# A two-layer diffusion backbone on one core: half-width sweeps ahead of the wide norms

## The reference

```python
def rms_norm(x, g):
    y = xf * lax.rsqrt(jnp.mean(xf * xf, axis=-1, keepdims=True) + EPS)
    return (y * g.astype(jnp.float32)).astype(x.dtype)
def swiglu(h, wg, wu, wd):
    return (jax.nn.silu(h @ wg) * (h @ wu)) @ wd
# layer
ada = lambda t, g, shift, scale: rms_norm(t, g) * (1 + scale) + shift
x = x + 0.5 * m(2) * ffn(ada(x, lp['norm_ffn1'], m(0), m(1)), 'ffn1')     # and xc, the context
y, yc = token_mix(ada(x, lp['norm_mix'], m(3), m(4)), ada(xc, ...), ...)  # w_in, four mixers, merge, w_out
x = x + m(5) * y
x = x + 0.5 * m(8) * ffn(ada(x, lp['norm_ffn2'], m(6), m(7)), 'ffn2')
```

## Time and profile before

| | |
|---|---|
| median of 3 runs | 2421.13 us (2415.59 to 2423.13) |
| profiled execution | 2425.87 us, span 2423.8 us |
| PE busy | 2273.6 us, 94% of the span |
| DVE busy | 1144.6 us, 47% |
| ACT busy | 863.2 us, 36% |
| POOL busy | 165.7 us, 7% |
| HBM | 322.86 MB moved by DMA, mean 133 GB/s |

### The profile page before, as it was taken

How to read it: one execution, slowest core, us unless ns; L and a number is a source line. 1 busy time by engine, 2 the same in 40 slices (tenths; PEclk the granted TensorE clock), 3 DMA queues, 4 the chain that set the end, 5 groups by cost and what they waited for, 6 DMA issues and landing times. The chain is left out here.

```text
span 2423.8 us, 33976 instructions
## 1 busy us (share of the span) xinstructions
PE 2273.6 (94%) x13093; PEld 1806.2 (75%) x13093; DVE 1144.6 (47%) x1847; ACT 863.2 (36%) x1350; POOL 165.7 (7%) x279
## 2 busy tenths in 40 slices
PE   4999998889999989899999989999998999988998
PEld 3777776768766767667777767788776877788997
DVE  1433332376377546543323244333336738775555
ACT  2322222243455442332222233223223446634443
POOL 2000000310000001000000000000013001110000
PEclk8999999989999999999999999999998999988999
DMA  9554636623333335255463635533363435564663
GB/s 270 154 159 113 171 108 184 183 70 90 87 97 100 95 100 164 71 140 166 115 173 110 170 107 140 157 96 96 105 168 80 114 97 147 145 177 140 179 181 110
DMA packets 584420, 322.86 MB, mean 133 GB/s; under 512 B 14666, under 2 KB 576310, under 8 KB 584150
## 3 DMA queue, kind: packets, MB, share of 16 engines
q1 hardware_dynamic: 570368, 288.40, 42.7%
q0 software_dynamic: 12464, 28.32, 4.3%
q10 hardware_dynamic: 1446, 4.18, 0.5%
HBM read 309.72 MB, written 12.94 MB: 133 GB/s over the span
## 5 line engine op out<-in xcount | busy, mean ns | idle before, releaser
L614 DVE TENSOR_TENSOR w_lo<-raw,w_hi 128x1024 fp32r<-128x1024 f32 (+1 forms) x412 | 497.8, 1209 | 1042.0 <-ACT w_hi L604 554.1
L604 ACT ACTIVATE w_hi<-raw 128x1024 fp32r<-128x1024 f32 (+1 forms) x412 | 428.5, 1040 | 966.4 <-PE bank L664 384.1
L663 PE MATMUL bank<-h_hi,w_hi 128*128 128x512 f32 (+1 forms) x1792 | 655.7, 376 | 13.2 <-DVE h_lo L1461 10.5
L664 PE MATMUL bank<-h_lo,w_hi 128*128 128x512 f32 (+1 forms) x1792 | 638.4, 366 | 0.0
L663 PEld LDWEIGHTS bank<-h_hi,w_hi 128*128 128x128 f32 x1792 | 343.1, 191 | 90.6 <-issue 35.2
L669 PE MATMUL bank<-h_hi,w_lo 128*128 128x512 f32 (+1 forms) x1792 | 393.1, 362 | 0.7 <-DVE w_lo L614 0.7
L664 PEld LDWEIGHTS bank<-h_lo,w_hi 128*128 128x128 f32 x1792 | 343.6, 192 | 52.0 <-issue 1.0
L669 PEld LDWEIGHTS bank<-h_hi,w_lo 128*128 128x128 f32 x1792 | 309.8, 190 | 52.2 <-DVE w_lo L614 1.1
L663 PE MATMUL bank<-inner_hi,w_hi 128*128 128x512 f32 (+1 forms) x704 | 254.0, 370 | 8.8 <-DVE inner_lo L1526 5.7
L664 PE MATMUL bank<-inner_lo,w_hi 128*128 128x512 f32 (+1 forms) x704 | 252.1, 368 | 0.0
L678 PE MATMUL bank<-h_hi,w_hi 128*128 128x512 f32 (+1 forms) x512 | 170.3, 351 | 13.2 <-ACT wa L1320 7.7
(11 more groups left out here) (226 smaller groups left out, 2258.7 us busy)
## 6 DMA issues: line engine op xcount, KB each, us to landing
raw<-in_w_mod_dram SPq DMA_DIRECT2D x144, 512.0 KB, 3.9
raw<-in_w_in_dram SPq DMA_DIRECT2D x108, 512.0 KB, 3.8
raw<-in_ffn_w_gate_dram SPq DMA_DIRECT2D x88, 512.0 KB, 4.9
raw<-in_ffn_w_up_dram SPq DMA_DIRECT2D x88, 512.0 KB, 5.0
raw<-in_ffn_w_down_dram SPq DMA_DIRECT2D x64, 512.0 KB, 4.0
raw<-in_ffn_w_down_dram SPq DMA_DIRECT2D x32, 384.0 KB, 3.7
raw<-in_w_branch_dram SPq DMA_DIRECT2D x16, 512.0 KB, 5.4
raw<-in_w_out_dram SPq DMA_DIRECT2D x16, 512.0 KB, 4.4
```

What stands on the lines that cost most here:

```text
L604: act.activation(w_hi[n % 2][:, 0:unit.rows, :], raw[unit.slot][:, 0:unit.rows, :], ACT.Copy).then_inc(hi_made, 1)
L614: dve.tensor_tensor(w_lo[n % 2][:, 0:unit.rows, :], raw[unit.slot][:, 0:unit.rows, :], w_hi[n % 2][:, 0:unit.rows, :].bitcast(F32), ALU.su ...
L663: pe.matmul(psum, w_hi[s][:, row0 + k, :], hi, start=(k == 0), stop=False)
L664: mm = pe.matmul(psum, w_hi[s][:, row0 + k, :], lo, start=False, stop=False)
```

## The change

Four of the six sweeps that a norm follows are done twice over, once for each token half: layer 0's last down sweep of the first block, its output projection, its last down sweep of the second block, and layer 1's last down sweep of the first block. Such a sweep has sixteen steps of 256 columns; the weights are loaded and split again for the second eight. During the second eight the norm of the first token half is worked: its sum after the ninth product, then root and reciprocal, then one chunk in each step. The first two products behind the norm run for the first token half and then for the second, and the sum of the second half stands inside them, after four steps. The adds of squares go to GpSimd, for every norm but the first. The first norm of the kernel is worked in two halves, one after the other. The parts are 8, 6 and 8 chunks, and the modulation units move accordingly. The vectors of the next modulation are made at step 6 of the sweep instead of 5.

```diff
-PARTS = [(0, 8), (8, 8), (16, 6)]
+PARTS = [(0, 8), (8, 6), (14, 8)]
-MOD_AT = {(0, 1, 0): (0, 16, 1), (0, 1, 1): (0, 32, 1), (0, 1, 2): (0, 48, 2),
+MOD_AT = {(0, 1, 0): (0, 16, 1), (0, 1, 1): (0, 32, 2), (0, 1, 2): (0, 56, 1),
...
+HALVED = [(0, (1, 2)), (0, "out"), (0, (2, 2)), (1, (1, 2))]
+def sweep_halves(l, name):
+    return 2 if (l, name) in HALVED else 1
+def sweep_steps(l, name):
+    return DC * sweep_halves(l, name)
...
-        TURN_AT = 5
+        TURN_AT = 6
...
+                        for again in range(sweep_halves(l, (ffn, part))):
+                            stage(first["down", l, ffn, part] + again * DC, DC, lambda j: [((0, n), columns(wd, l, j * P, n, c0))])
...
# TensorE, first_pair
+                for st in streams(n):
+                    cols = stream_cols(st)
+                    last = st == streams(n)[-1]
+                    for step in range(DC + 2):
+                        if (st, step) == (0, 4) and key != (0, 1) and n > LAT:
+                            sum_squares(key, 1)
...
+                            if which == 0:
+                                h_made.wait(pe, (*key, k, st))
+            def sum_squares(key, st):
+                cols = stream_cols(st)
+                (summed if key == (0, 1) else pooled).wait(pe, (key, DC - 2, st))
+                pe.matmul(sum_bank(key, st)[:, cols], const("ones"), wb[:, 1, cols], start=True, stop=False)
+                squares.wait(pe, (key, DC - 1, st))
...
# TensorE, between (after product d of a sweep)
+                if key and (l, name) in HALVED and d == DC:
+                    sum_squares(key, 0)
+                if key and (l, name) not in HALVED and d == DC - 1:
+                    sum_squares(key, 0)
...
# ScalarE, block_splits
+                for d in range(sweep_steps(l, name)):
...
                         act.wait_ge(added, add_first[l, name] + d + 1)
-                        square(key, n, d)
+                        square(key, d % DC, d // DC)
+                        if halved and d == DC:
+                            norm_root(key, 0)
+                        if halved and d >= DC:
+                            norm_hi(key, d - DC, 0)
...
-                norm_block(l, "mix", TOK, 1)
+                norm_block((l, "mix"), range(1, 2))
...
# VectorE, add_block
+                for d in range(sweep_steps(l, name)):
                     split_lo(dve, units[u0 + d].product + 2)
-                    if norm_key and d > 0:
-                        add_square(norm_key, norm_n, d - 1)
...
+                    for st in [d // DC] if halved else streams(n):
...
                     ins.then_inc(added, 1)
+                    if halved and d == DC:
+                        norm_invert(key, 0)
+                    if halved and d >= DC:
+                        norm_scale(key, d - DC, 0)
+                        if d > DC:
+                            norm_lo(key, d - DC - 1, 0)
+                if halved:
+                    norm_lo(key, DC - 1, 0)
...
# GpSimd
+            def add_squares(l, name):
+                key, n = next_norm(l, name)
+                for st in streams(n):
+                    squares.wait(pool, (key, 0, st))
+                    for k in range(1, DC - 1):
+                        squares.wait(pool, (key, k, st))
+                        if k > 1:
+                            pooled.wait(pool, (key, k - 1, st))
+                        before = wa[:, 0, stream_cols(st)] if k == 1 else wb[:, 1, stream_cols(st)]
+                        pooled.done(pool.tensor_tensor(wb[:, 1, stream_cols(st)], before, wa[:, k % 2, stream_cols(st)], ALU.add), (key, k, st))
...
                     load_modulation(0, "rest")
+                    add_squares(0, (1, 2))
                     neighbourhood_bias(0)
                     mixer_transfers(0)
+                    add_squares(0, "out")
```

More of the change, by code:

```diff
@@ L564, in _ @@
                                  ((0, DC), w_branch[l].rearrange("k (c p) n -> p (k c) n", p=P)[:, :, d * P:(d + 1) * P]))
-                        stage(first["out", l], DC, lambda j: [((0, DC), columns(w_out, l, j * P))])
+                        for again in range(sweep_halves(l, "out")):
+                            stage(first["out", l] + again * DC, DC, lambda j: [((0, DC), columns(w_out, l, j * P))])
                     for part, (c0, n) in enumerate(PARTS):
@@ L945, in _ @@
                             pe_start.done(mm, ("x", k))
-                    sum_squares((0, 1), TOK)
+                    for st in range(2):
+                        sum_squares((0, 1), st)
                     turn_modulation(0, "in")
@@ L1083, in _ @@
                 u0, a0 = first["out", l], add_first[l, "out"]
-                for d in range(DC):
+                for d in range(sweep_steps(l, "out")):
                     pe.wait_ge(added, a0 + d - 1)
+                    cols = stream_cols(d // DC) if (l, "out") in HALVED else slice(0, n)
                     if d == 0:
                         merged.wait(pe, (l, 6))
-                    product(u0 + d, 0, (0, 0), (bank[4 + d % 2][:, 0:n], 0, DC, h_rhs(n),
+                    product(u0 + d, 0, (0, 0), (bank[4 + d % 2][:, cols], 0, DC, lambda k: (h_hi[:, k, cols], h_lo[:, k, cols]),
                                                 (lambda k: h_made.wait(pe, (l, "merged", k))) if d == 0 else None))
@@ L1121, in root, with norm_root, norm_hi, norm_block @@
                 roots.done(act.activation(dst, psum, ACT.Sqrt, bias=eps_col[0:psum.shape[0], 0:1], scale=scale), key)
-            def norm_block(l, which, n, mod_i):
-                root((l, which), sums, (l, which), bank[6][:, 0:n], rstd[:, 0:n], 1.0 / D)
-                vectors.wait(act, (l, "in" if mod_i == 0 else "rest"))
-                for k in range(DC):
-                    normed.wait(act, (l, which, k))
-                    for st in streams(n):
-                        cols = slice(st * LAT, (st + 1) * LAT)
-                        ins = act.activation(h_hi[:, k, cols], wa[:, k % 2, cols], ACT.Identity,
-                                             bias=mod[:, 3 * mod_i * DC + k, st:st + 1])
-                    h_hi_made.done(ins, (l, which, k))
+            def norm_root(key, st):
+                root((key, st), sums, (key, st), sum_bank(key, st)[:, stream_cols(st)], rstd[:, stream_cols(st)], 1.0 / D)
+                if key[0] != "final":
+                    vectors.wait(act, (key[0], "in" if key[1] == 1 else "rest"))
+            def norm_hi(key, k, st):
+                normed.wait(act, (*key, k, st))
+                h_hi_made.done(act.activation(h_hi[:, k, stream_cols(st)], wa[:, k % 2, stream_cols(st)], ACT.Identity,
+                                              bias=mod[:, 3 * norm_vectors(key) * DC + k, st:st + 1]), (*key, k, st))
+            def norm_block(key, halves):
+                for st in halves:
+                    norm_root(key, st)
+                    for k in range(DC):
+                        norm_hi(key, k, st)
             def up(l, ffn, part, n):
@@ L1173, in block_splits @@
                 key, n = next_norm(l, name)
-                for d in range(DC):
+                halved = (l, name) in HALVED
+                for d in range(sweep_steps(l, name)):
                     if key and d == 0:
@@ new lines, in add_square_start, with norm_invert, norm_scale @@
+                    summed.wait(dve, ((0, 1), k - 1, 1))
+                    summed.done(dve.tensor_tensor(wb[:, 1, :], wb[:, 1, :], wa[:, k % 2, :], ALU.add), ((0, 1), k, 0))
+                summed.mark(((0, 1), k, 1))
+            def norm_invert(key, st):
+                roots.wait(dve, (key, st))
+                link(dve.reciprocal(rstd[:, stream_cols(st)], rstd[:, stream_cols(st)]))
+            def norm_scale(key, k, st):
+                if k >= 2:
+                    h_hi_made.wait(dve, (*key, k - 2, st))
+                    h_made.wait(dve, (*key, k - 2, st))
+                normed.done(dve.scalar_tensor_tensor(out=wa[:, k % 2, stream_cols(st)], in0=X[:, k, stream_cols(st)], scalar=gain[:, norm_vectors(key), k, st:st + 1],
+                                                     in1=rstd[:, stream_cols(st)], op0=ALU.mult, op1=ALU.mult), (*key, k, st))
@@ new lines, in norm_lo @@
+            def norm_lo(key, k, st):
+                normed.wait(dve, (*key, k, st))
+                h_hi_made.wait(dve, (*key, k, st))
+                h_made.done(dve.scalar_tensor_tensor(out=h_lo[:, k, stream_cols(st)], in0=wa[:, k % 2, stream_cols(st)],
+                                                     scalar=mod[:, 3 * norm_vectors(key) * DC + k, st:st + 1],
+                                                     in1=h_hi[:, k, stream_cols(st)].bitcast(F32), op0=ALU.add, op1=ALU.subtract), (*key, k, st))
@@ L1503, in up, with norm_block @@
+            def norm_block(key, halves):
+                for st in halves:
+                    norm_invert(key, st)
+                    for k in range(DC + 1):
```

(4 more changed lines are left out.)

147 lines of the change are left out of this document (61 added, 86 removed).

## The result

| | before | after |
|---|---|---|
| median (runs) | 2422.07 us (4) | 2438.64 us (4; 2437.79 to 2440.91) |
| profiled execution | 2425.87 us, span 2423.8 | 2439.42 us, span 2437.8 |
| TensorE busy | 2273.6 us | 2285.4 us |
| VectorE, ScalarE, GpSimd busy | 1144.6, 863.2, 165.7 us | 1172.0, 901.8, 210.7 us |
| moved by DMA | 322.86 MB | 339.78 MB |

The ratio is 1.0077, 95% interval 1.0060 to 1.0095. The forecast was +11.6 us; the profiled executions differ by 13.6 and the medians by 16.6. The median forecast was 2433 in a range of 2427 to 2440; 2438.64 lies near its upper end.

A forecast was written before the change was run, and what follows sets the result against it. TensorE was taken as the bound nearly everywhere, except 33.0 us of waits for norms' first chunks. Four halved sweeps with norms +11.3, start norm +3.8, layer 1's last block -3.5: +11.6 us, median 2433, range 2427 to 2440.

The forecast's parts named there:

- The ring of the halved sweeps: VectorE-ScalarE hand-overs pace halved sweeps: 3.05, once 6.34, then 3.61 us; 52.4 us from first residual add (X0) to sixteenth.
- Vectors: Next modulation's vectors, between a split and an add in the sweep: 1.7 us, about 1.1 in layer 1's first norm.
- From x to F: From the sixteenth add's start (x) to when the first product after the norm's first two can start (F): 17.9 us.
- The neighbourhood bias, "cost 0": Bias goes behind the sweep into the input projection, where TensorE has 5.4 us a product: cost 0.
- The part before: Second sweep of each feed-forward block ahead of a halved one, 8 chunks to 6: 10.3 us less.
- Ahead of the output sweep: Output projection's first split waits for a half-width instead of a full-width first product: about 2 us sooner.
- The start norm: Kernel's first norm in two halves, with vectors ahead of one reciprocal and the second between halves: +3.8 us.
- Layer 1's last block: At 256 columns: 6-chunk sweep without a norm 5.6 us less, last sweep longer; 3.5 us less in all.
- Splits did not run ahead: Rival: halved sweeps run at TensorE's pace, 44.8 us instead of 52.4, four times; 30 us less, 2403; chance 0.18.
- the clock stayed up: Rival: TensorE's clock stays high through the rest before the sixteenth add; four times 1.9 us less, 2425; chance 0.14.
- GpSimd did not meet the split: Third rival: GpSimd's adds of squares meet VectorE's w_lo splits in halved sweeps; 9.4 us more, 2442; chance 0.12.

The follow-up runs named there:

- the lull: The changed kernel with GpSimd's neighbourhood bias held until the input projection's first rotation is done, where VectorE is under half busy: 2429.06 us, ratio 1.0039.
- the first experiment: The changed kernel with GpSimd's neighbourhood bias waiting for the mixer norm's last h_lo chunk, so beside the convolutions: 2439.35 us, ratio 1.0093.
- the opened ring: The changed kernel with ScalarE's square and VectorE's scale one step later, h_hi and h_lo two: 2404.98 us, ratio 0.9935 to the kernel before.
- the start norm kernel: The changed kernel with both roots and both reciprocals of the start norm ahead of the vectors: 2432.89 us, ratio 1.0055 to the kernel before.

## Why the prediction was right, point by point

- *The ring of the halved sweeps.* Right: 3.05, 6.33 and 3.54 us for 3.05, 6.34 and 3.61. Opening it and changing the split's length moved the steps as a ring must.
- *Vectors.* 1.7 and 1.1 us expected, 1.07 and 0.79 measured (a step of 4.12 and one of 3.84 for 3.05). The reading of the earlier trace rows was at fault: at 492.52 to 494.20 GpSimd was still at the neighbourhood bias (until 493.9), and the four small instructions for the gains took 1.01 us. After the change GpSimd rests there and they take 0.40. Before and after:

```profile
492.99 1.01 DVE L1559 SCALAR_TENSOR_TENSOR gain<-mod,vec 128x8 f32<-128x8 f32 x4
...
479.27 0.40 DVE L1623 SCALAR_TENSOR_TENSOR gain<-mod,vec 128x8 f32<-128x8 f32 x4
```

- *From x to F.* The term of 17.9 was one number for four norms; measured were 23.9, 17.3, 19.8 and 21.9. Two things were mis-sized. The root was taken at x + 5.1 and stood at 6.1, 3.6, 6.2 and 5.0, as the clock fell or did not; the mean, 5.2, is close, each single norm is not. And in the mixer norms came 5.0 and 4.2 us that were not in the sum.
- *The neighbourhood bias, "cost 0".* This is the step that failed. The prediction put it into the input projection, where TensorE has 5.4 us a product. Its transfers began 1.7 us ahead of the last add and its arithmetic 9.9 us behind it, beside the second half's norm, where each chunk is a serial piece of the path; moved into the lull it gives back 9.6 us. And the place that the prediction named would have cost the same (the first experiment): what counts is VectorE's load, not TensorE's.
- *The part before.* 10.3 expected, 11.1 to 11.5 measured in three blocks. The 11.5 of layer 0 is the figure of one execution: the same gap, 377.2 us there, lay between 368 and 379 us in the other traces of kernels with these part sizes (last section).
- *Ahead of the output sweep.* 2.0 expected, 1.1 measured.
- *The start norm.* +3.8 expected, +4.2 measured from last gain to F.
- *Layer 1's last block.* -3.5 expected, -5.8 measured: the narrow output sweep also lost its add of squares, 23.43 to 21.38 us between first and last add, which the sum left out.
- *The rivals.* Splits did not run ahead; the clock stayed up in one norm of four in this execution. GpSimd did not meet the split: its adds took 0.73 to 0.86 us and w_lo stayed at 1.23. That rival's 9 us came from GpSimd all the same, at another place.

The sum was 2 us short in the profiled execution: about 9 missed for the bias, and 7 too many elsewhere. The ring, which carries most of the sum, was understood; that the other errors cancel to 2 us is luck: had only the bias been missed, the time would have been some 2442 us, outside the range.

## What to carry to other kernels

When two engines hand work to each other in program order, an idle time in front of each step is not slack. Write the cycle down hand-over by hand-over; shifting the dependent work one or two steps later gave 34 us, 23 in the steps and most of the rest behind the sweeps. When a GpSimd job is moved, look at what VectorE does at its new place, not at what TensorE does. And where TensorE rests ahead of such a stretch it can be worth feeding it, if only with products that nobody reads: 9.5 us here.

## What the runs showed of the hardware

- A GpSimd instruction with two inputs beside VectorE's scale and h_lo (both inputs in SBUF) stretches them from 0.48 to 0.77 and 0.94 us.
- Who pays depends on who came first, in the opened ring. In that trace 54 GpSimd adds began beside a split that was already running: the add took 1.40 to 1.61 us for 0.73, and the split kept its 1.21 to 1.23. One add, of 1015.02, began ahead of the split of 1015.35, and that split took 1.76. So there GpSimd does meet the split, as the third rival had it, and the add pays, off the path. Below are the row of an add that began behind a split (990.25, 1.22 us) and that of 1015.02, which itself had VectorE's scale of 1014.95 before it:

```profile
990.67 1.40 POOL L2008 TENSOR_TENSOR wb<-wa 128x256 f32<-128x256 f32 x1 [24.81 <-ACT wa L1155]
...
1015.02 1.02 POOL L2008 TENSOR_TENSOR wb<-wa 128x256 f32<-128x256 f32 x1 [8.54 <-ACT wa L1155]
```

- Much the same rest, 3.5 us in the mean, ended in a granted clock of 0.55, 1.00, 0.52 and 0.76 over the 7 us behind. Rests of 1.8, 1.4, 1.7 and 1.7 us in the opened ring ended in one fall and three without. What decides between them stays open.
- The stretch with two modulation units to a product differed between executions of the same instructions: from the first sweep's X0 to the second's 145.7 us in the profiled execution after, 137.3 in that of the start norm kernel. The granted clock goes with it, 0.94 in the mean against 1.00:

```profile
179.62:325.35 145.73, 132.22 (x862) 103.74 (x861) 37.77 (x49) 30.05 (x38) 6.63 (x12) 0.94 0.57 154
174.05:311.38 137.33, 124.95 (x862) 98.22 (x861) 37.78 (x49) 29.92 (x38) 6.63 (x12) 1.00 0.60 164
```

  Six per cent of 145.7 us is 8.7, and the difference is 8.4, so the clock accounts for it. It is a part of the spread of the runs, as large as half of the change's own effect; what makes the clock fall in some of them stays open.
